# The opening of a two-block network: modulation's scale ahead of its shift, and another order of the input slabs

## What is computed

```python
mod_l = (jax.nn.silu(c) @ w_mod[l] + b_mod[l])[:, None, :]
sh1, sc1, g1, sh2, sc2, g2 = jnp.split(mod_l, N_MOD, axis=-1)
pl = _modulate(_rmsnorm(xl, norm1_w[l]), sh1, sc1) @ w_in[l]    # h * (1 + scale) + shift
pc = _modulate(_rmsnorm(xc, norm1_w[l]), sh1c, sc1c) @ w_in[l]
qk = silu(dwconv2d(pl[..., :2 * W]))          # mLSTM queries and keys
v, o, gates = pl[..., 2 * W:3 * W], pl[..., 3 * W:4 * W], pl[..., 4 * W:]
out = head_rmsnorm(h, norm_w) * sigmoid(o)
```

## Time and profile before

| | us |
|---|---|
| median of 3 runs (3069.58 to 3070.26) | 3070.22 |
| the profiled execution | 3070.5 |
| its span in the profile | 3068.7 |
| PE busy | 3033.3 |
| first slab product of PE | 38.96 |
| first `nought` product of the heads | 164.34 |

### The profile page before, as it was taken

One profiled execution on the slowest core, in us unless ns is written; L12 is line 12 of the kernel. 1 busy time (PEld: TensorE's weight loads), 2 busy tenths in 40 slices (PEclk: granted clock), 3 DMA queues, 4 the chain that ended last, 5 costly groups with the idle time before them and its releaser, 6 DMA issues.

```text
span 3068.7 us, 38693 instructions
## 1 busy us (share of the span) xinstructions
PE 3033.3 (99%) x14587; PEld 2505.2 (82%) x14587; DVE 1336.2 (44%) x1576; ACT 582.4 (19%) x930; POOL 2034.7 (66%) x1499
## 2 busy tenths in 40 slices
PE   7999999999999999999999999999999999999999
PEld 5878978888888888877888888888888878888887
DVE  5763366887263322363353331333223653443321
ACT  4451252211120101231011100101001320111000
POOL 3515566888787767555777777777776546777764
PEclk9999999999999999999999999999999999999999
DMA  5201252222333323422233223333234222232222
GB/s 221 83 28 62 98 205 83 96 96 84 95 110 96 96 85 107 121 96 69 96 96 96 96 83 94 111 96 96 84 94 141 90 69 96 96 96 96 91 85 84
DMA packets 323078, 300.33 MB, mean 98 GB/s; under 512 B 6652, under 2 KB 316924, under 8 KB 319264
## 3 DMA queue, kind: packets, MB, share of 16 engines
q1 hardware_dynamic: 319056, 290.55, 29.6%
q10 hardware_dynamic: 3920, 8.36, 1.0%
HBM read 292.60 MB, written 2.10 MB: 96 GB/s over the span
## 4 chain that ended last, share of the span: by engine, by line
PE 95%; DVE 2%; DMA 1%; issue 1%; POOL 1%; ACT 1%; SPq 0%; DVEq 0%; POOLq 0%; ACTq 0%
PE pm L2269 25%; PE pm L2271 25%; PE pm L2270 25%; PE pa L2269 2%; PE pa L2270 2%; PE pa L2271 2%; PE pm L2338 1%; PE pm L2339 1%; PE pm L2340 1%; PE pm L2606 1%; PE pm L2299 1%; DMA modraw<-in_w_mod 1%; PE pa L2649 1%; PE pm L2303 1%; PE pa L2553 1%
## 5 line engine op out<-in xcount | busy, mean ns | idle before, releaser
L713 POOL TENSOR_TENSOR wlo<-raw,whi 128x512 fp32r<-128x512 f32 (+1 forms) x1088 | 1434.8, 1350 | 22.7
L709 POOL TENSOR_SCALAR whi<-raw 128x2048 fp32r<-128x2048 f32 (+1 forms) x272 | 478.4, 1759 | 941.8 <-PE pm L2271 597.6
L2269 PE MATMUL pm<-hh,whi 128*128 128x512 f32 x2280 | 894.6, 392 | 5.2 <-DVE mt L2232 2.8
L2271 PE MATMUL pm<-hh,wlo 128*128 128x512 f32 x2280 | 887.4, 389 | 0.0
L2270 PE MATMUL pm<-hl,whi 128*128 128x512 f32 x2280 | 887.4, 389 | 0.0
L2269 PEld LDWEIGHTS pm<-hh,whi 128*128 128x128 f32 x2280 | 428.0, 188 | 98.4 <-issue 5.7
L2270 PEld LDWEIGHTS pm<-hl,whi 128*128 128x128 f32 x2280 | 428.1, 188 | 90.6 <-issue 3.1
L2271 PEld LDWEIGHTS pm<-hh,wlo 128*128 128x128 f32 x2280 | 428.0, 188 | 89.8
L2269 PE MATMUL pm<-uh,whi 128*128 128x512 f32 x880 | 343.0, 390 | 0.7 <-POOL wlo L713 0.7
L2271 PE MATMUL pm<-uh,wlo 128*128 128x512 f32 x880 | 342.4, 389 | 0.0
L2270 PE MATMUL pm<-ul,whi 128*128 128x512 f32 x880 | 342.3, 389 | 0.0
(11 more groups left out here) (497 smaller groups left out, 3889.3 us busy)
## 6 DMA issues: line engine op xcount, KB each, us to landing
raw<-in_w_ffn SPq DMA_DIRECT2D x88, 1024.0 KB, 5.3
raw<-in_w_in SPq DMA_DIRECT2D x61, 1024.0 KB, 5.1
raw<-in_w_ffn SPq DMA_DIRECT2D x64, 704.0 KB, 4.4
raw<-in_w_up SPq DMA_DIRECT2D x22, 1024.0 KB, 5.0
raw<-in_w_out SPq DMA_DIRECT2D x12, 1024.0 KB, 5.0
raw<-in_w_down SPq DMA_DIRECT2D x16, 704.0 KB, 4.4
modbuf<-in_w_mod SPq DMA_DIRECT2D x10, 1024.0 KB, 5.1
modraw<-in_w_mod SPq DMA_DIRECT2D x8, 1024.0 KB, 19.5
```

What stands on the lines that cost most here:

```text
L709: nc.gpsimd.tensor_scalar(h, r, 1.0, 1.0, ALU.mult, ALU.mult).then_inc(hi_done, 1)
L713: last = nc.gpsimd.tensor_tensor(o[:, c], r[:, c], h[:, c].bitcast(F32), ALU.subtract)
L2269: nc.tensor.matmul(out, wh, ah, start=start, stop=False)
L2271: return nc.tensor.matmul(out, wl, ah, start=False, stop=stop)
```

## The change

- The modulation's weights come in two halves: the eight scale halves right behind x, then the first two slabs, then, once the scale has landed, the eight shift halves and the context.
- PE multiplies the scale halves alone (`opening_part(k, 0)`), after 72 idle products, and turns them; DVE forms x times scale times the reciprocal root (`scaled_x`), ACT and DVE split it into `hh` and `hl` without the shift.
- Slab 0 is now the second output-gate slab. It is multiplied with these `hh` and `hl`; the shift halves' products (`opening_part(k, 1)`) are set between its k 2 to 5, and their turn behind k 6. Then PE multiplies the shift by the slab's weights (`opening_shift`), turns the result, and ACT adds it as a bias when it copies the slab to `mo`.
- `hh` and `hl` are made a second time, with the shift, behind slab 0. Slab 1 (queries 0) follows them k by k (`slab_second`). The context's squares, root, `ch` and `cl` come after them, and the context's squares are added by one reduction over k of `csq`.
- The order is now: output gate 1, queries 0, output gate 0, two gate slabs, values 0, queries 1, keys 0, keys 1, values 1, with other PSUM halves. The sigmoids are taken early (`output_gate` between the context's k 4, 5 and 6, and one over 1024 columns). `values(0)` moves behind the gates' activations on ACT, `conv(1)` behind the gate steps on DVE; keys are centred when their latent half is multiplied; the first scores move into the context part of the last slab.
- Semaphore counts and some tiles' places follow.

The core of the diff:

```diff
-IN1 = ([("mq", 0), ("mv", 2 * ML_W), ("gate", 0), ("gate", 1), ("mq", SLAB), ("mo", 3 * ML_W), ("mk", ML_W),
-        ("mk", ML_W + SLAB), ("mv", 2 * ML_W + SLAB), ("mo", 3 * ML_W + SLAB)]
+IN1 = ([("mo", 3 * ML_W + SLAB), ("mq", 0), ("mo", 3 * ML_W), ("gate", 0), ("gate", 1), ("mv", 2 * ML_W), ("mq", SLAB), ("mk", ML_W),
+        ("mk", ML_W + SLAB), ("mv", 2 * ML_W + SLAB)]
...
-MV_AT, GATE_AT, MO_AT, CONV_SLABS = (1, 8), 2, (5, 9), (0, 4, 6, 7)
+MV_AT, GATE_AT, MO_AT, CONV_SLABS = (5, 9), 3, (2, 0), (1, 6, 7, 8)
 IN1_SLABS = len(IN1)
...
-    p_ = (0, 1, 0, 0, 1, 0, 1, 0, 1, 0)[i_] if i_ < 10 else i_ % 2
+    p_ = (0, 1, 0, 0, 0, 1, 0, 1, 0, 1)[i_] if i_ < 10 else i_ % 2
...
+                sp.dma_start(modraw[k][:, 0:D], wm[k][:, D:2 * D]).then_inc(mod_loaded[MOD_GROUP[k]], 16)
             sp.dma_start(raw[0][:].rearrange("p k n -> p (k n)"), io["w_first"]).then_inc(raw_loaded[0], 16)
+            sp.dma_start(raw[1][:], slab_view(io["w_in"], 0, IN1[1][1])).then_inc(raw_loaded[1], 16)
+            for g in range(4):
+                sp.wait_ge(mod_loaded[g], 16 * MOD_GROUP.count(g))
+            for k in range(KD):
+                sp.dma_start(modraw[k][:, D:2 * D], wm[k][:, 0:D]).then_inc(mod_loaded[k // 2], 16)
+            sp.dma_start(cx[:].rearrange("p k t -> p (k t)"), io["ctxT"]).then_inc(ctx_loaded, 16)
...
+                    sp.wait_ge(opening, OPENING_ADDED)
...
+                opening_rstd(0, std, T)
+                act.wait_ge(opening, 1)
+                nc.scalar.activation(modrow[0][:, 0:D // 4], pm[1][:, 0, 0:D // 4], ACT.Copy).then_inc(mod_in, 1)
+                for k in range(KD):
+                    act.wait_ge(xn_done, k + 1)
+                    nc.scalar.activation(hh[:, k, :], pa[2 + k % 2][:], ACT.Copy).then_inc(hh_done, 1)
...
+                act.wait_ge(ctx_loaded, 16)
+                act.sem_inc(sq_done, KD - 2)
+                for e in range(2):
+                    some = slice(KD // 2 * e, KD // 2 * e + KD // 2)
+                    nc.scalar.activation(csq[:, some, :], cx[:, some, :], ACT.Square).then_inc(sq_done, 1)
...
-                for n, (src, hi, w) in enumerate(((xn, hh, T), (cx, ch, CT))):
-                    act.wait_ge(xn_done, KD * n + KD)
-                    if n:
-                        act.wait_ge(hn_done, KD // 2)
-                    for k in range(KD):
-                        nc.scalar.activation(hi[:, k, :], src[:, k, :], ACT.Identity, bias=mod_col(0, k, n), scale=wsc[:, n, k:k + 1]).then_inc(hh_done, 1)
...
+                for k in range(KD):
+                    act.wait_ge(hn_done, k + 1)
+                    if k < KD - 1:
+                        act.wait_ge(opening, OPENING_TURNED + k + 1)
+                    else:
+                        act.wait_ge(slab_used, 2 + 1)
+                    nc.scalar.activation(hh[:, k, :], pa[2 + k % 2][:], ACT.Identity, bias=mod_col(0, k)).then_inc(hh_done, 1)
+                    if k == 0:
+                        act.wait_ge(opening, OPENING_ADDED)
+                        nc.scalar.activation(mo_row[:], pa[1][:, 0:SLAB], ACT.Copy).then_inc(mod_in, 1)
+                    if k == 4:
+                        act.wait_ge(mod_done, 4)
+                        for e in range(2):
+                            nc.scalar.activation(mo[:, 2 + e, :], pm[0][:, e, :], ACT.Identity, bias=mo_shift[:, e:e + 1]).then_inc(mod_in, 1)
+                        act.wait_ge(mod_in, 6)
+                        act.sem_inc(pm_free[0], 1)
+                opening_rstd(1, rstd, CT)
+                def output_gate(e):
+                    if e:
+                        act.wait_ge(slab_used, 2 + MO_AT[0] + 1)
+                    else:
+                        act.wait_ge(opening, MO_HALF)
+                    nc.scalar.activation(mo[:, e, :], pm[0][:, e, :], ACT.Sigmoid).then_inc(mod_in if e else pm_free[0], 1)
+                for k in range(KD):
+                    if k in (5, 6):
+                        output_gate(k - 5)
+                    act.wait_ge(hn_done, KD + k + 1)
+                    nc.scalar.activation(ch[:, k, :], pa[2 + k % 2][:, 0:CT], ACT.Identity, bias=mod_col(0, k, 1)).then_inc(hh_done, 1)
+                nc.scalar.activation(mo[:, 2:4, :], mo[:, 2:4, :], ACT.Sigmoid).then_inc(mod_in, 1)
...
-                    act.wait_ge(slab_used, 2 + i + 1)
+                    if is_k:
+                        act.wait_ge(opening, KEYS_MULTIPLIED[c - 2])
+                    else:
+                        act.wait_ge(slab_used, 2 + i + 1)
...
-                    for t, ctx_ in ((0, False), (0, True), (1, True), (1, False)) if is_k else ((0, False), (1, False)):
+                    for t, ctx_ in ((0, False), (1, False), (0, True), (1, True)) if is_k else ((0, False), (1, False)):
...
                 centre(0)
-                values(MV_AT[0], 0)
                 conv_out(0)
...
+                values(MV_AT[0], 0)
                 centre(1)
                 conv_out(1)
-                output_gate(0)
                 centre(2)
...
-                        if h == 0 and i == 1:
-                            output_gate(1)
-                            nc.scalar.preload_act_table_set("natural_log_exp_and_others")
...
                 conv(0)
-                conv(1)
...
+                conv(1)
                 conv(2)
...
+                def scaled_x(k, done):
+                    nc.vector.scalar_tensor_tensor(pa[2 + k % 2][:], x[:, k, :], wsc[:, 0, k:k + 1], pa[0][:], ALU.mult, ALU.mult).then_inc(done, 1)
...
+                def scaled_ctx(k):
...
+                scaled_x(0, xn_done)
+                for k in range(KD):
+                    if k < KD - 1:
+                        if k:
+                            v.wait_ge(hl_done, k)
+                        scaled_x(k + 1, xn_done)
+                    v.wait_ge(hh_done, k + 1)
+                    nc.vector.tensor_tensor(hl[:, k, :], pa[2 + k % 2][:], hh[:, k, :].bitcast(F32), ALU.subtract).then_inc(hl_done, 1)
+                for k in range(2):
+                    v.wait_ge(hl_done, KD - 1 + k)
+                    scaled_x(k, hn_done)
+                v.wait_ge(mod_turned, 1)
+                turned, bias = mod_turned_of(0)
+                nc.vector.tensor_tensor(modc[:, 0:KD, :].rearrange("p (g t) j -> p t g j", t=2), turned, bias, ALU.add).then_inc(mod_done, 1)
                 v.wait_ge(mod_done, 3)
...
+                    v.wait_ge(hh_done, KD + k + 1)
+                    nc.vector.scalar_tensor_tensor(hl[:, k, :], pa[2 + k % 2][:], mod_col(0, k), hh[:, k, :].bitcast(F32), ALU.add, ALU.subtract).then_inc(hl_done, 1)
+                    if k < KD - 2:
+                        v.wait_ge(hl_done, KD + k + 1)
+                        scaled_x(k + 2, hn_done)
+                v.wait_ge(sq_done, 2 * KD)
+                v.sem_inc(sq_added, KD - 1)
+                nc.vector.tensor_reduce(rstd[:, 0:CT], csq[:].rearrange("p k t -> p t k"), mybir.AxisListType.X, ALU.add).then_inc(sq_added, 1)
...
+                    v.wait_ge(hn_done, KD + k + 1)
+                    v.wait_ge(hh_done, 2 * KD + k + 1)
+                    nc.vector.scalar_tensor_tensor(cl[:, k, :], pa[2 + k % 2][:, 0:CT], mod_col(0, k, 1), ch[:, k, :].bitcast(F32), ALU.add, ALU.subtract).then_inc(hl_done, 1)
+                    if k < KD - 2:
+                        v.wait_ge(hl_done, 2 * KD + k + 1)
+                        scaled_ctx(k + 2)
...
+                    last.then_inc(opening, 1)
+                    if 2 <= k < 6:
+                        next(shift)
+                        next(shift)
+                    if k == 6:
+                        pe.wait_ge(mod_row, 1)
+                        opening_turn(1, pm[1][:, 1, 0:2 * KD]).then_inc(mod_turned, 1)
...
+                for k in range(KD):
+                    g = k % 4
+                    last = nc.tensor.matmul(pa[1][32 * g:32 * g + 32, 0:SLAB], modc[:, k, 0:1].to_broadcast([P, 32]), raw[0][:, k, :], start=k < 4, stop=k >= 4)
...
+                            opening_sum(1, rstd, CT)
...
                         last = nc.tensor.matmul(pm[use][:, i, :], o[:, k, c], hh[:, k, :], start=False, stop=k == KD - 1)
+                    if i == 0:
+                        last.then_inc(opening, 1)
...
+                    if t and mid:
+                        mid()
...
+                idle(72)
                 pe.wait_ge(mod_in, 1)
-                for k, _ in enumerate(modulation(0, KD)):
+                for k in range(KD):
+                    pe.wait_ge(mod_loaded[MOD_GROUP[k]], 16 * MOD_GROUP.count(MOD_GROUP[k]))
+                    last = opening_part(k, 0)
                     if k == 3:
-                        square_sum(1, rstd, CT)
-                    if k == 6:
+                        opening_sum(0, std, T)
+                    if k in (5, 6):
                         idle(4)
-                pe.wait_ge(mod_row, 1)
-                mod_turn(modrow[0], pm[1][:, 1, :])
-                idle(5)
```

(57 more changed lines are left out.)

190 lines of the change are left out of this document (97 added, 93 removed).

## The result

The changed kernel takes 3082.32 us (median of 6 runs, 3081.31 to 3085.97) against 3070.24 (3069.3 to 3070.72, 6 runs beside it): 1.0042 times as long, 95% interval 1.0029 to 1.0055. That is +12.1 us; the forecast was 3077.8, +7.6. The direction and the range held, the size did not. The profiled execution took 3081.63 us with a span of 3079.8.

What follows compares the result with a forecast made beforehand. The kernel was taken as one queue of PE work behind an opening. Terms -5.3 + 5.7 + 5.0 + 0.9 + 1.3 = +7.6 us made the span 3076.3, and with 1.5 outside it 3077.8 us; range 3072.0 to 3083.0.

Steps and rivals of the forecast that it cites:

- (a): Opening: slab 0 starts at 33.7 instead of 38.96, set by the end of the idle products; -5.3 us.
- (b): Shift products, turns and context sum move from the opening's load waits into PE's stream between slabs; +5.7 us, bounds 5.2 and 7.3.
- (c): At slab 5 (values), PE waits until DVE's convolution of the queries gives back pm[1]; +5.0 us, bounds 4.3 and 6.
- (d): PE waits for POOL's split of the keys' slab, slowed beside DVE's gate steps; +0.9 us, bounds 0 and 2.
- (e): Before the heads, PE waits for both copies of the last slab, the second values; +1.3 us, bounds 0.8 and 1.7.
- the one without a wait at slab 5: Rival: pm[1] comes back in time for slab 5; +2.6 us, 3072.8 us, no measurable change; chance 0.15.
- the one with a real gain: Rival: slab 0 starts much earlier or moved products overlap, and (c) is absent; 3067.3 us or some 3 less; chance 0.06.
- The change does what it says: Denies a rival: loads come as before, slab 0 starts near 39, +12.9 us, 3083.1 us; chance 0.05.
- strided sum: Rival: the stride doubles DVE's reduction of the context's squares to 4.4 us; PE waits 1.1 in slab 2, 3078.9 us; chance 0.12.

Runs made afterwards that it cites:

- e3_idle52: The changed kernel with 52 idle products at the start instead of 72; 3077.6 us.
- e2_conv: The changed kernel with the queries' convolution, the first centre and the first output gate moved early in ACT's and DVE's order; 3077.3 us.
- e7_group: The changed kernel with the eight shift products in slab 0 in two blocks of four instead of four pairs; 3080.1 us (single run).
- e8_block: The changed kernel with all eight shift products in one block behind the sixth k of slab 0 instead of four pairs; 3080.4 us (single run).
- e1_fill: The changed kernel with sixteen idle products added between the gate slabs and slab 5, in PE's wait; 3079.7 us.
- e5_vals: The changed kernel with ACT copying the context's part of the last slab's values before the latents' part; 3081.3 us (single run).
- c2_all: The changed kernel with 44 first idle products, fewer later ones, the convolution early, the values' context part first, shift blocks of two, two, four; 3068.35 us.

## Why the prediction was right, and where not

- **(a)**, start of slab 0, -5.3: the mechanism holds (e3_idle52), the size is -4.3 in the profiled execution. Of the missing 1.0, 0.6 is the end of the first idle products (23.4 for 22.8): they began at 4.09 for 3.8 and took 19.3 for 19.0, and both change from one execution to the next; in e2_conv slab 0 did start at the 33.7 forecast. The 19.0 was right in part by luck: the slow stretch was longer than read from the earlier trace rows, 27 records in the 5.9 us up to 10 instead of 13 in 3.2, and the rest quicker, 0.113 us apart instead of 0.12. The other 0.4 is the way from there to slab 0, 11.3 us for the 10.9 that I added up. On it the eight scale products, in four blocks between others, took 4.0 for the 3.4 of the sum, the error of (b) once more, and the fourteen idle ones 3.1 for 3.4.
- **(b)**, PE work moved into the stream, +5.7: **this is the step that failed.** It measured +7.9, above its upper bound of 7.3. The prediction costed each moved product as half of a 512-column one, 0.43 us, and that is right. It left out that the products stood in blocks that break into a run of another kind: 0.38 us for each block (e7_group, e8_block), four times in slab 0, which is 1.5 of the 2.2 that were missing. The other 0.7 lies at the two turns, the shift times the gate slab and the context's sum (0.8 us in slab 2 for the 0.4 forecast); that these pay for their breaks too is likely, but no run took them out. The rows of before had these products only in the opening, among waits for loads, where a break is hard to see.
- **(c)**, the wait at slab 5, +5.0: 4.5, released by the step named, gone with the order named (e2_conv). DVE and ACT had pm[1] free 13.0 us after slab 2 for the 13.4 forecast. Missing was what the wait does afterwards, the second thing that the sum lacked: a clock at half for nearly 4 us, +1.3 in the profiled execution and up to 2.7 in others (e1_fill, e8_block). All eight profiles with this wait have the tail, and e1_fill, in which PE was kept busy, has none. The earlier trace rows had shown the slow first products behind the 18 us of waiting, and I used them for the start alone.
- **(d)**, splits beside the gate steps, +0.9: 0. The contention was there (9.4 us of split, not the over 10 that was to show it), but the stall of (c) had carried PE past the worst of it. Without the stall it was 0.8 (e2_conv). Two terms that I had added exclude each other in part.
- **(e)**, the values' copies, +1.3: 1.4, and 0.9 of it comes back with the order of two instructions (e5_vals).

Sum of the differences: +1.0, +2.2, -0.5 + 1.3, -0.9, +0.1, and 0.4 that the account doesn't place: +3.6, which leads from 7.6 to 11.2. (The bounds added up to +13.2 and not to +13.5; it moves no conclusion.)

Of the rivals, the one without a wait at slab 5 and the one with a real gain fell with the wait and with slab 0's start at the end of the idle products. The change does what it says: SP, which holds the shift's loads back until the scale has landed, issued them from 21.9 on, and the scale's products ran from 23.3, before the shift was there. The **strided sum** was right as a mechanism and small as a price. DVE took 3.87 us, between the contiguous 2.3 and the 4.4 assumed, and PE waited 0.2 us. The Trainium skill, SBUF — State Buffer, section Door 1: The DMA port swizzle, has the rule that steps to new 16-byte lines cost; 2.28 in order against 3.87 with the stride agrees with it, and ACT's strided writes (4.18 against 2.00) behave alike.

## What to carry to other kernels

Work moved from a place where the engine waits into its running stream costs more than its own duration: count the breaks, and put small products of another kind in one block. When two stages are to share a buffer in a new order, follow the buffer's release through the written order of every engine that uses it; here the convolution taken early would have saved 3.7 us, nearly what the reordered loads brought (4.3). And when filler work covers a load, its count has to follow when the load is made shorter: the scale came earlier, and some 23 of the 72 idle products stood in its way (an estimate from c2_all, where 28 fewer left a wait of 1.2 us, five such products).

## What the hardware showed that was not expected

- PE idle for 4.5 us in the middle of a run came back at half pace (products of 256 columns 0.213 us apart, then 0.12) for 3.6 to 6.8 us, a cost of 1.3 to 2.7; filled with idle products, the same place had none of it.
- The same 144 first idle products took from 17.89 to 19.27 us in nine profiles: the slow part at the start has no fixed length. With the tail it would explain why the changed kernel's times spread over 4.7 us, why two of e3_idle52's nine took 3080.5 and 3080.7, 3 us above its median, and why those of c2_all, which has the slow start but no tail, spread over 1.1; that was not tried by itself.
- A block of 128 x 32 products into 32-row groups, set into a run of full products, costs 0.38 us beside its products, the change there and back together, whether it shows 16, 32 or 64 records.
